# A state-space layer rewritten in chunks of four tokens, its chunk matrices built during the feed-forward network before it

## The chip, the cores and the metric

The kernel runs on one core of one Trainium2 chip. The metric is the device time of one execution in microseconds. The engines are named as the profile names them: PE (TensorE), DVE (VectorE), ACT (ScalarE), POOL (GpSimd) and SP (SyncE, which only issues DMAs here).

## The reference, cut to what matters

Two blocks run one after the other on 256 tokens of width 1024. The second has four layers, each a mixer followed by a SwiGLU feed-forward network (FFN): forgetting attention ("fox"), S5, a pooling layer, fox again. The S5 layer is what the change rewrites:

```
u = h @ w_in                                # 256 x 1024, 64 groups of 16 channels
lam_bar = exp(lam * dt)                     # complex, 64 groups x 64 states
b_bar = ((lam_bar - 1) / lam) * b
bu = b_bar u                                # 16 channels -> 64 states in each group
state_t = lam_bar * state_{t-1} + bu_t      # over the 256 tokens
y = Re(c state) + d * u
g = gelu(y);  val, gate = split(g @ w_glu);  x = x + val * sigmoid(gate)
```

## The kernel before, in words

Activations lie transposed in SBUF, features over the partitions in KC = 8 tiles of 128 rows and T = 256 columns (tokens). Weights stream through two rings of four buffers that SP fills: `ring` with tiles of 1 MB, `dring` with down projections of 0.5 MB. A product of fp32 precision is made of three fp32r matmuls (`mm3`, lines 644 to 646): weights are split into a high half by ACT (`make_high`, line 1248; `make_down_high`, line 1254) and a low half by DVE (`make_low`, line 380; `make_down_low`, line 389). Nothing plans the order at run time: each engine has its own program, and semaphores join them.

An FFN has 22 slices. PE (`swiglu`) issues for slice j first `gate_up(j + 2)`, 48 matmuls, and then `down(j)`, 24 matmuls. ACT's part of slice j is: wait for the scaled sums of j, SiLU (line 1499), `make_high(j + 2)`, `make_down_high(j + 1)`. The last of these waits until PE has done `down(j - 1)`, since there are two buffers:

```
if d >= HIGH or not isinstance(g, int):
    act.wait_ge(sem("down_free"), d - HIGH + 1 + RING * g)
```

DVE scales the sums (line 2099), makes the hidden activations (2102 to 2106), the low half of tile j + 2 and of down tile j + 1, and in slices 1 to 5 of the FFN in front of S5 also a part of `s5_matrices`, which scales B (lines 2269 to 2275, six operations of 256 elements).

The S5 layer: PE projects u with four tiles (`s5in`), DVE scales it (line 2282). Then 32 columns j of 128 states follow. For each, PE multiplies B with u (line 1145, 2 matmuls of 256 tokens), DVE rotates into a frame in which the recurrence is real (lines 2298 to 2302), runs two scans over 256 tokens (line 2306), rotates back (2310 to 2312), leaving the two products of each part apart, and PE sums them in PSUM while it multiplies with C (line 1161, 4 matmuls). Line 1155 adds d * u. The rotations are tables of 256 tokens for four columns, doubled eight times by POOL (`rotations`, lines 591 to 598) in two buffers: the first two are made during the attention of layer 0, the others while the scan runs, each when DVE has left the buffer. After every four columns ACT applies gelu to a tile of 128 outputs (line 1568) and makes its high half (1570), DVE the low half (2315), and PE runs the GLU, 16 groups of 24 matmuls on eight tiles.

## Time and profile before

| | |
|---|---|
| median of 3 runs | 2737.49 us (2734.57 to 2745.36) |
| the profiled execution's own time | 2734.69 us |
| its span in the profile | 2733.0 us |
| busy in the span | PE 2280.9, DVE 1724.9, ACT 1079.3, POOL 735.9 us |
| mean granted clock of PE | 0.90 of full speed |

The profile is one execution. "Busy" is the time in which an engine had an instruction running; a wait is put down to what released it. A clock of 1.00 is 2.4 GHz, 0.50 is 1.2 GHz. The stages around the change follow each other so: attention of layer 0 until about 1438 us, its output projection, FFN0 from 1467 to 1653, the S5 projection until 1682, the scan until 1896, the GLU until 1949.

### The profile page before, as it was taken

The numbers are of one execution on the slowest core, as the hardware profiler recorded it, in microseconds if no ns is written. First come the engines' busy times: TensorE is split into PE (matmuls) and PEld (weight loads), VectorE is DVE, ScalarE is ACT, GpSimd is POOL, SyncE is SP. The second block draws the span as 40 slices with busy tenths as digits, with TensorE's granted clock in tenths as the row PEclk, the third lists the DMA queues.
The fourth block names the chain that finished last, engine by engine and source line by source line (L and its number), as shares of the span: only waits on it lengthen the run. The fifth ranks groups of instructions, "written<-read, shape, count | busy, mean of one in ns | idle before, by whom it ended". The sixth has DMA issues, their size and how long they took to land.

```text
span 2733.0 us, 40794 instructions
## 1 busy us (share of the span) xinstructions
PE 2280.9 (83%) x15156; PEld 1926.7 (70%) x15160; DVE 1724.9 (63%) x2631; ACT 1079.3 (39%) x1527; POOL 735.9 (27%) x522
## 2 busy tenths in 40 slices
PE   5998768688678865875999997667999699999997
PEld 2864545677466555764969996224999599887997
DVE  3488463477458545765557667997666766654665
ACT  3221533376432534664444333001433333445432
POOL 2320032488452135883240000783000000000000
PEclk7995889899788888997999998777999899999999
DMA  5248702499526125995415452000545244442442
GB/s 232 93 185 323 246 0 107 185 341 343 209 77 234 44 88 205 323 321 185 160 42 202 174 208 77 0 0 31 185 184 200 100 162 184 164 152 72 175 184 92
DMA packets 93046, 443.72 MB, mean 162 GB/s; under 512 B 9088, under 2 KB 25600, under 8 KB 56704
## 3 DMA queue, kind: packets, MB, share of 16 engines
q1 hardware_dynamic: 79104, 390.10, 39.1%
q0 software_dynamic: 8496, 31.99, 3.0%
q10 hardware_dynamic: 5328, 20.04, 1.8%
q8 instruction: 76, 1.25, 0.2%
q14 instruction: 42, 0.34, 0.0%
HBM read 401.20 MB, written 40.89 MB: 162 GB/s over the span
## 4 chain that ended last, share of the span: by engine, by line
PE 39%; DVE 6%; POOLq 2%; POOL 2%; ACT 2%; DVEq 2%; issue 1%; DMA 0%; ACTq 0%
PE bank L645 12%; PE bank L644 11%; PE bank L646 11%; DVE ring_halves L380 2%; POOLq L593 1%; ACT high L1248 1%; POOLq L598 1%; PE bank L1098 1%; POOL XT L591 1%; PE bank L1075 1%; PE bank L1088 1%; DVEq L2301 1%; PE bank L1161 1%; POOL XT L594 1%; PE bank L686 1%
## 5 line engine op out<-in xcount | busy, mean ns | idle before, releaser
L644 PE MATMUL bank<-ssdb_halves,high 128*128 128x256 f32 (+1 forms) x2080 | 613.2, 295 | 62.3 <-DVE HT_halves L1683 34.9
L645 PE MATMUL bank<-HT_halves,high 128*128 128x256 f32 (+1 forms) x2096 | 623.7, 298 | 0.0
L646 PE MATMUL bank<-ssdb_halves,ring_halves 128*128 128x256 f32 (+1 forms) x2080 | 612.3, 294 | 0.0
L380 DVE TENSOR_TENSOR ring_halves<-ring,high 128x2048 fp32r<-128x2048 f32 (+1 forms) x200 | 414.8, 2075 | 157.7 <-ACT high L1248 157.5
L1248 ACT CAST high<-ring 128x2048 fp32r<-128x2048 f32 x230 | 437.2, 1903 | 134.1 <-PE bank L646 134.1
L380 POOL TENSOR_TENSOR ring_halves<-ring,high 128x1024 fp32r<-128x1024 f32 (+1 forms) x96 | 363.6, 3789 | 375.3 <-ACT high L1248 375.3
L644 PEld LDWEIGHTS bank<-ssdb_halves,high 128*128 128x128 f32 x2080 | 398.3, 192 | 81.9 <-issue 55.1
L645 PEld LDWEIGHTS bank<-HT_halves,high 128*128 128x128 f32 x2096 | 398.9, 190 | 9.1
L646 PEld LDWEIGHTS bank<-ssdb_halves,ring_halves 128*128 128x128 f32 x2080 | 394.6, 190 | 9.7
L389 DVE TENSOR_TENSOR dring_halves<-dring,dhigh 128x1024 fp32r<-128x1024 f32 (+1 forms) x152 | 226.0, 1487 | 154.7 <-ACT dhigh L1254 148.5
L1254 ACT CAST dhigh<-dring 128x1024 fp32r<-128x1024 f32 x152 | 160.5, 1056 | 238.2 <-PE bank L646 238.1
L644 PE MATMUL bank<-border_halves,dhigh 128*128 128x256 f32 x704 | 198.4, 282 | 9.1 <-DVE border_halves L2106 9.1
L646 PE MATMUL bank<-border_halves,dring_halves 128*128 128x256 f32 x704 | 198.1, 281 | 0.0
L645 PE MATMUL bank<-border_halves,dhigh 128*128 128x256 f32 x704 | 198.0, 281 | 0.0
L646 PE MATMUL bank<-high,HT_halves 128*128 128x256 f32 x640 | 182.7, 285 | 0.0
L644 PE MATMUL bank<-high,HT_halves 128*128 128x256 f32 x512 | 156.8, 306 | 17.9 <-POOL ring_halves L380 11.0
L1161 PE MATMUL bank<-wide,zs_b 128*32 128x256 f32 x256 | 94.5, 536 | 68.0 <-DVE wide L2312 67.9
L645 PE MATMUL bank<-ring_halves,HT_halves 128*128 128x256 f32 x512 | 145.6, 284 | 0.0
L644 PEld LDWEIGHTS bank<-border_halves,dhigh 128*128 128x128 f32 x704 | 133.3, 189 | 9.8 <-issue 9.8
L645 PEld LDWEIGHTS bank<-border_halves,dhigh 128*128 128x128 f32 x704 | 133.4, 189 | 0.0
L646 PEld LDWEIGHTS bank<-border_halves,dring_halves 128*128 128x128 f32 x704 | 133.2, 189 | 0.0
L644 PE MATMUL bank<-HT_halves,high 128*128 128x256 f32 (+1 forms) x384 | 117.9, 307 | 9.5 <-DVE MIX_halves L1903 8.4
(426 smaller groups left out, 4384.1 us busy)
## 6 DMA issues: line engine op xcount, KB each, us to landing
ring<-in_ffn SPq DMA_DIRECT2D x88, 1024.0 KB, 5.4
ring<-in_moe SPq DMA_DIRECT2D x64, 1024.0 KB, 7.5
ring<-in_ada SPq DMA_DIRECT2D x48, 1024.0 KB, 7.0
dring<-in_ffn_down SPq DMA_DIRECT2D x88, 512.0 KB, 3.5
dring<-in_moe_down SPq DMA_DIRECT2D x64, 512.0 KB, 4.6
ring<-in_foxin SPq DMA_DIRECT2D x24, 1024.0 KB, 4.8
ring<-in_win SPq DMA_DIRECT2D x22, 1024.0 KB, 4.8
zs_b<-x_slots POOLq DMA_DIRECT2D x32, 512.0 KB, 8.6
```

The costliest lines, as they stand in the source:

```text
L380: eng.tensor_tensor(low, w, h, ALU.subtract).then_inc(sem(f"low_{engine}"), 1)
L389: eng.tensor_tensor(low, w, h, ALU.subtract).then_inc(sem(f"down_low_{engine}"), 1)
L591: ptt(new, low, cos, ALU.mult)
L593: pool.drain()
L594: ptt(new[:, 0], new[:, 0], tmp[:, 1], ALU.subtract)
L598: pool.drain()
L644: mm(o, a[0], b[0], start=first, stop=last and bool(kw), **kw)
L645: mm(o, a[0], b[1], start=False, stop=last and bool(kw), **kw)
L646: return mm(o, a[1], b[0], start=False, stop=last, **kw)
L1161: i = mm(y, cT[:, part, j, :], z, start=False, stop=n == 3, skip_group_check=True, tile_position=(0, q))
L1248: nc.scalar.copy(r(high[c % HIGH][:]), ring[t % RING][:]).then_inc(sem("high"), 1)
L1254: nc.scalar.copy(r(dhigh[d % HIGH][:]), dring[d % RING][:]).then_inc(sem("down_high"), 1)
```

## The change

The tokens are taken in 64 chunks of four. A state is carried from chunk to chunk only, so a column of 128 states has 64 steps in place of 256, and one DVE instruction now works on four columns at once: there are 8 of them (c), of 256 elements as before. PE forms the input of a chunk from its four tokens with the powers of lam times B (8 matmul calls of 128 weights and 64 columns per c), the outputs of the four tokens from the state before the chunk with C times the powers (8 calls), and what the tokens of a chunk do to each other with a 128 x 128 matrix per column that also holds d (4 calls). DVE adds the two products of the rotation itself (one more addition of 512 elements per c).

The matrices are built in FFN0, whose loops are written out in full on PE, ACT and DVE. In slices 1 to 16 DVE makes one power of B or C per slice (two halves of 16 columns, four steps of B and four of C each), in slices 5 to 8 and 13 to 16 ACT spreads the powers of B into block form and PE transposes them, which ACT copies back, in slices 9 to 12 and 17 to 20 ACT does the same with C and PE multiplies C with B to give the sums inside a chunk. POOL doubles two tables of 64 rotations for 16 columns each (six levels, products of up to 1024 elements), and stores everything with its DMAs in DRAM. In the S5 layer SP loads for each c a tile of 1 MB (B and C) and one of 0.5 MB (the matrix in the chunk and the rotations), and moves u into chunk order and gelu(y) back, in four moves of 16 DMAs of 32 partitions by 1 KB. POOL no longer works during attention and scan; a 32 x 63 product makes the decay (`fade`). The B and C arrays in DRAM are half as large, and the four transposes and ACT copies ahead of the S5 projection and the skip matrix on DVE are gone. Two GLU low halves that DVE made ahead of the scan are made behind it. The first two groups of the GLU are interleaved on PE. ACT does not begin layer 1 before the last matrix is stored.

```diff
+            def s5_moves(t0):
+
+                def tables(c):
+                    if c < RING:
+                        sp.wait_ge(sem("down_free"), DOWN_AT["ffn", 0] + FFN_SLICES)
+                    else:
+                        sp.wait_ge(*at("s5_pe", ("out", c - RING)))
+                    sp.dma_start(dring[c % RING][:], s5_kr[c]).then_inc(*done(f"s5_kr{c % RING}", c, 16))
+                    load(t0 + c, s5_bc[c])
+
+                def move(half, dst, src, key):
+                    for s_ in range(STEP):
+                        for q in range(BATCH):
...
+                            sp.dma_start(dst(s_, q, half), src(s_, q, half)).then_inc(*done(f"moved{half}", key, 16))
...
+                for n in ("s5_bt_kept", "s5_c_kept", "s5_k_kept0", "s5_k_kept1", "s5_loaded"):
+                    sp.wait_ge(*at(n, "last"))
+                for c in range(2):
+                    tables(c)
+                sp.wait_ge(*at("s5_dve", ("u_sb", 3)))
+                move(0, to_rel, from_nat, "u")
+                for c in range(2, RING):
+                    tables(c)
+                sp.wait_ge(*at("s5_dve", ("u_sb", KC - 1)))
+                move(1, to_rel, from_nat, "u")
+                for c in range(RING, KC):
+                    tables(c)
+                sp.wait_ge(*at("s5_act", ("y", 3)))
+                move(0, to_nat, from_rel, "y")
...
+            def s5_keep_out(c):
+                pool.wait_ge(*at("s5_act", ("e_blk", c)))
+                for i in range(2):
+                    pool.dma_start(s5_bc[c][:, (2 + i) * BATCH * P:(3 + i) * BATCH * P].rearrange("p (b c) -> p b c", b=BATCH),
+                                   e_blk[:, i, :, 1:, :].rearrange("p b s c -> p b (s c)"))\
+                        .then_inc(*done("s5_c_kept", c if c < KC - 1 else "last", 16))
...
+                s5_turns(0)
+                for half in range(2):
+                    for c in range(BATCH * half, BATCH * half + BATCH):
+                        s5_keep(c)
+                    if half == 0:
+                        pool.wait_ge(*at("s5_loaded", "rot"))
+                        s5_turns(1)
+                    for c in range(BATCH * half, BATCH * half + BATCH):
+                        s5_keep_out(c)
+                        if c > BATCH * half:
+                            s5_keep_k(c - 1)
+                    s5_keep_k(BATCH * half + BATCH - 1)
@@ PE @@
+                half, c = j // 13, (j - 5) % 4 + 4 * (j // 13)
+                if 5 <= j <= 8 or 13 <= j <= 16:
+                    pe.wait_ge(*at("s5_act", ("x_blk", c)))
+                    for q in range(BATCH):
+                        for i in range(2):
+                            mm_ = nc.tensor.transpose(ps[6 + q // 2][:, (2 * (q % 2) + i) * P:(2 * (q % 2) + i + 1) * P],
+                                                      x_blk[:, i, q].rearrange("p s c -> p (s c)"), ident)
+                    mm_.then_inc(*done("s5_pe", ("turned", c)))
+                c = (j - 9) % 4 + 4 * (j // 17)
+                if 9 <= j <= 12 or 17 <= j <= 20:
+                    pe.wait_ge(*at("s5_act", ("e_blk", c)))
+                    pe.wait_ge(*at("s5_dve", ("e", c // 4)))
+                    for q in range(BATCH):
+                        o = ps[6 + c % 2][0:QUAD, q * P:q * P + P]
+                        for i in range(2):
+                            mm(o, b_one[:, i, (BATCH * c + q) % S5_HALF, :], e_blk[:, i, q, 0:STEP, :], start=q == 0 and i == 0,
+                               stop=False, skip_group_check=True)
+                        mm_ = mm(o[:, 0:QUAD], ident[:, 0:QUAD], skip_diag[:, (BATCH * c + q) % S5_HALF, :], start=False, stop=True,
+                                 skip_group_check=True)
+                    mm_.then_inc(*done("s5_pe", ("k_sums", c)))
...
+                if build is not None:
+                    for j in range(slices):
+                        build(j)
+                        if j + 2 < slices:
+                            gate_up(j + 2, 0)
+                        down(j, 0)
+                    return
...
+                    w = ring[t % RING][:, 0:2 * BATCH * P].rearrange("p (b a s) -> p b a s", b=BATCH, a=2)
                     for i in range(2):
-                        mm_ = mm(ps[j % 2][:, i * T:i * T + T], bT[q:q + 32, i, c, :], Q2[q:q + 32, c, :],
-                                 start=True, stop=True, tile_position=(q, 0))
-                    mm_.then_inc(sem("bu"), 1)
-
-                def outputs(j):
-                    q, c = 32 * (j % 4), j // 4
-                    bank = ps[2 + c % 2]
-                    if j % 4 == 0:
-                        if c >= 2:
-                            pe.wait_ge(*at("s5_y", c - 2))
-                        mm(bank[:, 0:T], s5_dmat[:, c, :], Q2[:, c, :], start=True, stop=False, skip_group_check=True)
-                    pe.wait_ge(sem("states_done"), j + 1)
-                    y = bank[q:q + 32, 0:T]
-
-                    for n, (part, z) in enumerate(((0, s5_q[:, j % 2, 0, 0, :]), (0, s5_q[:, j % 2, 1, 0, :]),
-                                                   (1, s5_q[:, j % 2, 0, 1, :]), (1, s5_q[:, j % 2, 1, 1, :]))):
-                        i = mm(y, cT[:, part, j, :], z, start=False, stop=n == 3, skip_group_check=True, tile_position=(0, q))
-                    i.then_inc(sem("s5_out"), 1)
+                        for q in range(BATCH):
+                            mm_ = mm(ps[c % 2][:, i * T + q * CHUNKS:i * T + q * CHUNKS + CHUNKS], w[:, q, i, :], u_rel[:, q, c, :],
+                                     start=True, stop=True)
+                    mm_.then_inc(*done("s5_pe", ("in", c)))
+
+                def outputs(c):
+                    w = ring[(t0 + c) % RING][:, 2 * BATCH * P:].rearrange("p (a b s) -> p a b s", a=2, b=BATCH)
+                    pe.wait_ge(*at(f"s5_kr{c % RING}", c))
+                    if c < 2:
+                        pe.wait_ge(*at("s5_dve", ("u_sb", KC - 2 + c)))
+                    else:
+                        pe.wait_ge(*at("s5_act", ("y", c - 2)))
+                    y = ps[2 + c % 2]
+                    for q in range(BATCH):
+                        mm(y[:, q * CHUNKS:q * CHUNKS + CHUNKS], dring[c % RING][:, q * P:q * P + P], u_rel[:, q, c, :],
+                           start=q == 0, stop=False, skip_group_check=True)
+                    pe.wait_ge(*at("s5_dve", ("states_done", c)))
+                    for q in range(BATCH):
+                        for part in range(2):
+                            z = s5_q[:, c % 2, 0, part, q * CHUNKS:q * CHUNKS + CHUNKS - 1]
+                            mm_ = mm(y[:, q * CHUNKS + 1:q * CHUNKS + CHUNKS], w[:, part, q, :], z,
+                                     start=False, stop=part == 1, skip_group_check=True)
+                    mm_.then_inc(*done("s5_pe", ("out", c)))
+                    pe.drain().then_inc(sem("tile_free"), 1)
 
                 inputs(0)
-                for j in range(S5_CH):
-                    if j + 1 < S5_CH:
-                        inputs(j + 1)
-                    outputs(j)
+                for c in range(KC):
+                    if c + 1 < KC:
+                        inputs(c + 1)
+                    outputs(c)
@@ ACT @@
+                def turned(c):
+                    act.wait_ge(*at("s5_pe", ("turned", c)))
+                    if c:
+                        act.wait_ge(*at("s5_bt_kept", c - 1))
+                    for i in range(2):
+                        copied = nc.scalar.copy(b_turned[:, 2 * i:2 * i + 2], ps[6 + i][:].rearrange("p (b a s) -> p b a s", b=2, a=2))
...
+                    q = BATCH * (c % BATCH)
+                    for g in range(2):
+                        rows = slice(64 * g, 64 * g + 64)
+                        nc.scalar.copy(x_blk[rows, :, :, :, 16 * g:16 * g + 16].rearrange("p a b s c -> p a (b s) c"),
+                                       x_pow[rows, :, q:q + BATCH].rearrange("p a b s c -> p a (b s) c"))
+                        copied = nc.scalar.copy(b_one[rows, :, q:q + BATCH, 16 * g:16 * g + 16], x_pow[rows, :, q:q + BATCH, STEP - 1, :])
+                    copied.then_inc(*done("s5_act", ("x_blk", c)))
...
+                def out_blocks(c):
+                    act.wait_ge(*at("s5_dve", ("e", c // BATCH)))
+                    if c:
+                        act.wait_ge(*at("s5_pe", ("k_sums", c - 1)))
+                        act.wait_ge(*at("s5_c_kept", c - 1))
+                    q = BATCH * (c % BATCH)
+                    for g in range(2):
+                        rows = slice(64 * g, 64 * g + 64)
+                        nc.scalar.copy(e_blk[rows, :, :, 0, 16 * g:16 * g + 16], e_one[rows, :, q:q + BATCH])
+                        for i in range(2):
+                            copied = nc.scalar.copy(e_blk[rows, i, :, 1:, 16 * g:16 * g + 16], e_pow[rows, i, q:q + BATCH])
+                    copied.then_inc(*done("s5_act", ("e_blk", c)))
+
+                if 6 <= j <= 9 or 14 <= j <= 17:
+                    turned((j - 6) % 4 + 4 * (j // 14))
+                if 10 <= j <= 13 or 18 <= j <= 21:
+                    sums((j - 10) % 4 + 4 * (j // 18))
+                if 5 <= j <= 8 or 13 <= j <= 16:
+                    blocks((j - 5) % 4 + 4 * (j // 13))
+                if 9 <= j <= 12 or 17 <= j <= 20:
+                    out_blocks((j - 9) % 4 + 4 * (j // 17))
...
+                    if build is not None:
+                        build(j)
...
+                    act.wait_ge(*at("s5_pe", ("out", c)))
+                    act_fn(g_rel[:, :, c, :], ps[2 + c % 2][:, 0:T].rearrange("p (b t) -> p b t", b=BATCH), ACT.Gelu_apprx_tanh)\
+                        .then_inc(*done("s5_act", ("y", c)))
+                    if c >= 5:
+                        gelu_high(c - 5)
+                    if c == 6:
+                        make_high(SPLIT_AT["glu", 1])
+                gelu_high(3)
+                make_high(SPLIT_AT["glu", 1] + 1)
+                for c in range(BATCH, KC):
+                    gelu_high(c)
@@ DVE @@
+                def times(x, re, im, out, conj):
+                    f_re, f_im = (pv(i)[:, own].unsqueeze(1).unsqueeze(3).to_broadcast([P, 2, S5_HALF, 16]) for i in (re, im))
+                    a, b = s5_tmp
+                    tt(a, x, f_re, ALU.mult)
+                    tt(b, x, f_im, ALU.mult)
+                    dve.drain()
+                    tt(out[:, 0], a[:, 0], b[:, 1], ALU.add if conj else ALU.subtract)
+                    return tt(out[:, 1], a[:, 1], b[:, 0], ALU.subtract if conj else ALU.add)
...
+                step = j - 1 if j < 9 else j - 9 if j < 17 else 8
...
+                elif step < STEP:
+                    i = times(x_pow[:, :, :, STEP - step, :], 18, 19, x_pow[:, :, :, STEP - 1 - step, :], False)
+                    if step == STEP - 1:
...
+                    q = s5_q[:, c % 2]
+                    if c >= 2:
+                        dve.wait_ge(*at("s5_pe", ("out", c - 2)))
+                    tt(q[:, 0], s5_z, cos2, ALU.mult)
+                    stt(q[:, 1, 0], s5_z[:, 1], -1.0, sin, ALU.mult, ALU.mult)
+                    tt(q[:, 1, 1], s5_z[:, 0], sin, ALU.mult)
+                    dve.drain()
+                    tt(q[:, 0], q[:, 0], q[:, 1], ALU.add).then_inc(*done("s5_dve", ("states_done", c)))
+                make_low(dve, "dve", SPLIT_AT["glu", 1])
+                for c in range(KC):
+                    dve.wait_ge(*at("s5_act", ("gelu_high", c)))
+                    y = y_nat[:, :, c // BATCH, CHUNKS * (c % BATCH):CHUNKS * (c % BATCH) + CHUNKS]
+                    tt(r(by_step(O2r[:, c, :])), y, by_step(H2r[:, c, :]), ALU.subtract).then_inc(*done("s5_dve", ("gelu_split", c)))
+                    if c == BATCH - 1:
+                        make_low(dve, "dve", SPLIT_AT["glu", 1] + 1)
```

## Rows read from the trace of the kernel before

**Rows 1.** Windows: stretch, length, busy us of PE, PEld, DVE, ACT, POOL, clock, DMA share.

```profile
1467.40:1653.10 185.70, 180.46 (x1522) 179.60 (x1521) 125.91 (x158) 69.78 (x65) 0.00 (x0) 1.00 0.47 177
...
1682.40:1895.80 213.40, 140.25 (x403) 61.94 (x401) 194.80 (x298) 9.09 (x17) 131.53 (x192) 0.73 0.01 5
...
1311.60:1437.60 126.00, 117.92 (x794) 98.39 (x793) 62.05 (x127) 54.48 (x120) 45.23 (x68) 0.95 0.27 93
2381.00:2506.00 125.00, 117.88 (x793) 98.58 (x792) 58.43 (x126) 54.41 (x120) 0.00 (x0) 0.95 0.26 93
```

**Rows 2.** Timeline of DVE over the first column: start us, us, engine, line, operation.

```profile
1689.88 0.69 DVE L2298 TENSOR_TENSOR wide<-bank,XT 128x512 f32<-128x512 f32 x1 [2.22 <-PE bank L1145]
1690.49 0.41 DVE L2299 TENSOR_TENSOR wide<-bank,XT 128x256 f32<-128x256 f32 x1
...
1694.83 0.68 DVE L2298 TENSOR_TENSOR wide<-bank,XT 128x512 f32<-128x512 f32 x1
```

**Rows 3.** POOL: tables' last six levels (timeline), and contended products by form.

```profile
1382.52 0.24 POOL L591 TENSOR_TENSOR ssdb<-ssdb,arow 128x32 f32<-128x32 f32 x1
...
1394.69 1.89 POOL L592 TENSOR_TENSOR sig<-ssdb,arow 128x1024 f32<-128x1024 f32 x1
...
1397.95 1.28 POOL L595 TENSOR_TENSOR ssdb<-ssdb,sig 128x512 f32<-128x512 f32 x1
...
L592 POOL TENSOR_TENSOR sig<-XT,arow 128x1024 f32<-128x1024 f32 x3 | 7.0, 2340 | 0.0
```

**Rows 4.** Timeline of PE: the eight output instructions of two columns.

```profile
1882.43 1.91 PE L1161 MATMUL bank<-wide,zs_b 128*32 128x256 f32 x8 [0.31 <-DVE wide L2312]
...
1892.28 3.62 PE L1161 MATMUL bank<-wide,zs_b 128*32 128x256 f32 x8 [1.78 <-DVE wide L2312]
...
1895.84 0.58 PE L644 MATMUL bank<-HT_halves,high 128*128 128x256 f32 x1
```

**Rows 5.** Timeline of DVE: third and fourth u of the S5 projection.

```profile
1670.42 0.75 DVE L2282 TENSOR_TENSOR HT<-bank,rstd 128x256 f32<-128x256 f32 x2
```

**Rows 6.** DMA issues (KB each, us to landing) and timelines of SP and POOL issuing.

```profile
zs_b<-x_slots POOLq DMA_DIRECT2D x32, 512.0 KB, 8.6
...
ring<-in_glu SPq DMA_DIRECT2D x8, 1024.0 KB, 4.8
...
473.05 0.33 SPq L422 DMA_DIRECT2D ring<-in_moe  x1
473.42 0.44 SPq L427 DMA_DIRECT2D dring<-in_moe_down  x1
...
1458.26 0.60 POOL L627 DMA_DIRECT2D MIX<-in_s_b  x1 [59.03 <-DVE XT L1922]
```

**Rows 7.** Timeline of ACT over one slice of FFN0.

```profile
1543.26 1.05 ACT L1254 CAST dhigh<-dring 128x1024 fp32r<-128x1024 f32 x1 [2.95 <-PE bank L646]
1546.46 0.42 ACT L1499 ACTIVATE border<-wide 128x256 f32<-128x256 f32 x1 [2.15 <-DVE wide L2099]
1546.78 1.90 ACT L1248 CAST high<-ring 128x2048 fp32r<-128x2048 f32 x1
1551.76 1.05 ACT L1254 CAST dhigh<-dring 128x1024 fp32r<-128x1024 f32 x1 [3.08 <-PE bank L646]
```

**Rows 8.** FFN0: waits (total us, times, longest); groups by form, 1468 to 1665.

```profile
ACT dhigh L1254 <- PE bank L646: 55.3, 20, 3.2
...
PE bank L644 <- DVE ring_halves L380: 2.9, 2, 1.6
...
L1557 ACT COPY MIX<-bank 128x512 f32<-128x512 f32 x3 | 1.5, 584 | 0.0
```

**Rows 9.** Windows behind two gaps of PE, columns as in Rows 1.

```profile
2389.80:2392.40 2.60, 0.06 (x2) 0.06 (x1) 2.53 (x3) 1.71 (x1) 0.00 (x0) 1.00 0.77 246
2393.00:2396.50 3.50, 3.50 (x19) 3.50 (x18) 1.43 (x1) 0.00 (x0) 0.00 (x0) 0.51 0.13 52
...
1668.00:1671.40 3.40, 0.75 (x6) 0.78 (x7) 3.40 (x5) 1.90 (x1) 0.00 (x0) 1.00 0.67 231
1671.40:1675.00 3.60, 3.60 (x33) 3.60 (x32) 2.40 (x2) 0.00 (x0) 0.00 (x0) 1.00 0.19 77
```

353 lines of the change are left out of this document (206 added, 147 removed).

## The prediction

> **What bounds the kernel now.** I read the stages first, as windows of the span [rows 1]. The first FFN of the second block (FFN0, 1467 to 1653 us) has PE busy 180.5 of 185.7 us: PE is the bound. The stretch from the end of the S5 input projection to the GLU (1682.4 to 1895.8, 213.4 us) has DVE busy 194.8 us, PE 140 at a mean granted clock of 0.73, and POOL 132. There DVE works through 32 columns; undisturbed, one takes 4.95 us from start to start [rows 2], but 32 of them would be 158 us, so some 50 us are waits and contention with POOL, which makes the rotation tables of the next four columns: a contended 1024-element product there takes 2.34 us, a clean one 1.89 [rows 3]. PE's outputs end the stage: 8 matmul instructions in 3.62 us at the low clock, 1.91 at the high one [rows 4], and the GLU starts at 1895.8.
>
> **What goes and what comes.** The scan shrinks from 32 columns to 8 (four tokens per step), and everything a chunk needs (the powers of B and C, the kernel inside a chunk, the 64-step rotations) is built during FFN0 by DVE, ACT, PE and POOL and kept in DRAM. Two costs have to be told apart: the new S5 stage, and FFN0, where the building is put on a stage that PE bounds.
>
> **1. The new S5 stage.** Count from the end of FFN0, 1653.1. Before, the GLU starts at +242.7 [rows 1]. After:
> - PE still projects until about +29 [rows 1]. The first move to chunk order needs the fourth u, which DVE has at 1671.2, +18 [rows 5]; it is 16 small DMAs on SP. Two issues of SP stand 0.37 us apart, one takes 0.33 to 0.44 [rows 6]; at 0.45 each 7.2 us, and a landing of 2.5 to 4 (the nearest, 1 MB, is 4.8 [rows 6]): done at +29, under the projection. First column at +32, against +36.8 before [rows 2].
> - One column on DVE: 4.95 plus a drain and one 512-element addition (0.69, of which 0.61 to the next start [rows 2], and some 0.15 for the drain), so 5.7. PE has 20 matmul calls of 64 columns in it, 40 instructions; 0.11 us each at the high clock is 4.5 us, at the low one 8 to 9 (an estimate: a quarter of the 0.24 and 0.45 per 256 columns of [rows 4], doubled for the load of 128 weights beside so few columns). PE would bind at the low clock only; I take 6.1 per column, 8 of them 49 us. Bounds 5.7 and 8: 46 and 64.
> - Tail, all on the path: last outputs 3, gelu 0.5, the last move 16 x 0.45 = 7.2 and 2.5 to land, ACT's and DVE's splits 2. Less 5 us of GLU matmuls that the two interleaved first groups have done by then. A move bounded by 0.37 and 1.0 per issue is 6 to 16.
> - Sum: 32 + 49 + 3 + 0.5 + 7.2 + 2.5 + 2 - 5 = +91. Saved: 242.7 - 91 = **151.5 us**.
>
> SP is also passed by 12 MB of tables (8 x 1.5 MB). Tables 0 to 3 come under the projection; table c waits for outputs of c - 4 and has four columns, 24 us, to land; 1 MB takes 4.8 [rows 6]. Hidden; if it were not, every column would wait some 2 us. GLU tiles load from the fifth output on, hidden too; the fourth comes behind the last move but has 17 us. The two low halves of GLU tiles that DVE makes ahead of the scan (2.28 each) move behind it, one under the last outputs, one under the last move, where DVE has nothing else. The skip matrix (1.2 us) and the four transposes ahead of the scan go. Fox0's attention loses POOL's tables: that stage was 126.0 against 125.0 for its twin without them [rows 1], gain 1.
>
> **2. FFN0, per slice.** Today a slice is 8.5 us of PE (two ACT casts of dhigh start 1543.26 and 1551.76) [rows 7]. ACT's cast of the next down weights must wait for PE's down(j-1): 55.3 us of such idle [rows 8]. The new helper is called on ACT behind this cast, and on PE directly behind down(j-1), in front of gate_up(j+2). So for j = 5 to 20 PE stands still until ACT has done the cast and its copies. What was slack of ACT becomes a wait of PE. Sixteen times:
> - cast 1.05 [rows 7] plus three hand-overs at 0.1 = 1.35: **21.6 us**.
> - ACT's copies: 512 elements 0.58 [rows 8], 256 0.42, the next starting 0.1 before the end [rows 7]; 128 elements an estimate of 0.25. State blocks 1.5, output blocks 1.8, turned 1.0, sums 0.5: 8 x 1.5 + 8 x 1.8 + 8 x 1.0 + 7 x 0.5 = **38 us**.
> - PE's own: 64 transposes, one instruction of 128 columns each, 0.12 by halving the 0.24 per 256 columns of [rows 4], 8 us; 64 calls of 128 columns (two instructions each) and 32 of 32 columns, 16 us: **24 us**.
> - A single wait for POOL. ACT has one buffer of output blocks and overwrites it in slice 10 only when POOL's DMA of the first one has landed; POOL issues that after the second half's rotations, which it begins after slice 9's turned blocks. They are the six last levels of today's eight, 16.7 us clean (1382.52 to 1399.23), up to 1.24 times as much beside DVE [rows 3], say 19.5; then six DMA issues at 0.57 and a landing. POOL's 512 KB land in 8.6 us in the MoE [rows 6]; I take 4.5 for 256 KB. Blocks free at 2.2 + 0.6 + 19.5 + 3.4 + 4.5 = 30 after down(8); ACT would be there at 17.5 (a slice of 16 and 1.6 for cast and sums): **12.5 us** (6 to 20).
> - The clock. PE would now stand 2.9 to 4.2 us in each of 16 slices. Behind a 2.5 us gap at 2389.8 it ran 3.4 us at 0.51, 1.2 GHz; behind a similar gap at 1668 it stayed at 1.00 [rows 9]. A low stretch costs half of itself, 1.7. Six in ten: **17 us** (0 to 27).
> - DVE: each step (two 512- and two 256-element operations) equals the old ones in slices 1 to 4, which cost 2.9 us of PE [rows 8]. From slice 5 on it lies under the longer slice. Zero net; without that cover 1 us per slice. The loop written out over 22 slices issues the same matmuls, as the other stages that are written out do; zero.
>
> Sum **113 us**. Behind FFN0 ACT waits for the last kernel DMA, 1 us.
>
> The Trainium skill (DMA: Bandwidth & Descriptors, "Anatomy of one DMA — SWDGE (gpsimd) path") gives a DMA of GpSimd about 2.0 us fixed plus its bytes at 436 GB/s, against this change with its 64 moves and 80 stores. By it 256 KB would land in 2.6 us and the POOL wait would be 10.6, which makes the sum 2 us less; no row here shows so small a DMA, and the nearest, 8.6 us for 512 KB, is far above it.
>
> **Total.** -151.5 - 1 + 113 + 1 = -38.5. Against the profiled execution's 2734.7 (span 2733.0) that is 2696; its run lies 2.8 under the median of 2737.5, so **2699 us**.
>
> **Rivals.**
> - *FFN0 hides more.* The clock stays up and POOL's wait is short: 17 + 8 less; the copies overlap better, 5 less. 2669. For: the gap at 1668 did not lower the clock. Against: PE's order is fixed, the cast can't come earlier.
> - *The S5 stage is PE's or SP's.* Columns of 8 us at the low clock (+15) and moves of 1 us per issue (+9, both moves) or late tables (+6): +30, 2729. For: clock 0.73 in this stage today. Against: DVE's 5.7 leaves PE 1 us of slack at the high clock.
> - *Slower: the clock in FFN0.* If PE's standing in each slice keeps it at 1.2 GHz through slices 5 to 20, and not for one stretch of 3.4 us, each slice's 8.5 us of matmuls becomes 17: 16 x 8.5 = 136 in place of 17, 2818. The change turns slower from about 40 us above my sum, which is 23 more low stretches than my ten, two per slice. For: the scan stage ran at 0.73 with PE busy two thirds. Against: here PE works over 10 us on end between two waits, and at 2393 one 3.4 us stretch was enough. The skill's page "TensorE: Matmul & The Clock Gate", section "HAM oscillation — how this bites in real kernels", tells of a loop whose wait in each turn puts PE back to the low clock each time; by that rule all 16 slices pay 1.7, 27 us, and the time is 2709, inside my forecast.
> - *It does not shorten the scan's bound*: the stage is held by table traffic. 12 MB at four times the landing rate of one MB is 58 us, no more than the columns; 2710. Hardly distinct.
>
> **Chances.** Forecast with its neighbourhood (2680 to 2718) 0.55; more hidden (below 2680) 0.18; S5 stage longer (2718 to 2751) 0.18; slower by FFN0's clock 0.09. A measurement of this kernel tells about 0.5% from no change, 14 us: faster below 2723.8 is 0.55 + 0.18 + a third of 0.18 = 0.79; within 0.12; slower 0.09. Range 2660 to 2736: it leaves out a part of the clock rival and a tail on the other side.
>
> **What would show it.** Right: FFN0 some 300 us long, PE idle in slices 5 to 20 in front of the transposes and sums, released by ACT's copies, 3 to 4 us each; one wait of ACT for a DMA near slice 10, 10 us or more; DVE's columns 5.7 to 6.3 us apart, eight of them; 15 us between the last column and the GLU's full pace. Wrong: FFN0 below 270 or above 330 us; columns over 7 us; PE waiting for tiles of the tables.

## The result and the profile after

The kernel after takes 2749.05 us (median of 7 runs, 2745.08 to 2756.84), the kernel before 2737.49: a ratio of 1.0044, 95% interval 1.0025 to 1.0063. The forecast was 2699, faster; the change made the kernel 0.4% slower. The profiled execution took 2745.08 us with a span of 2743.3, against 2733.0 before.

Where it went, by the reciprocals that open a stage (rstd, VectorE's timeline), the first slice of FFN0 and its last matmul (1653.1 before, 1787.1 after):

| stretch | before | after | difference | forecast |
|---|---|---|---|---|
| start to rstd of fox0 | 1311.65 | 1305.64 | -6.0 | 0 |
| to rstd of FFN0 | 155.7 | 155.2 | -0.6 | -1 |
| FFN0, first slice to last matmul | 182.7 | 323.3 | +140.6 | +113 |
| from there to the S5 rstd | 12.6 | 12.4 | -0.2 | +1 |
| S5 rstd to rstd of FFN1 | 287.2 | 157.8 | -129.4 | -151.5 |
| the rest | 780.0 | 786.0 | +5.9 | 0 |

The first and the last line (work that the change leaves alone) cancel; why each moved by 6 us is not shown. The change saves 129.4 us in the S5 stage and pays 140.6 for it in FFN0.

Windows of the kernel after, columns as in [rows 1]: FFN0, the scan from its first column to just before the last outputs, and the last move.

```profile
1463.80:1787.10 323.30, 242.96 (x1754) 233.62 (x1752) 159.74 (x201) 106.33 (x168) 87.36 (x123) 0.83 0.41 140
1819.80:1885.00 65.20, 60.18 (x287) 58.93 (x285) 42.92 (x80) 4.38 (x10) 0.00 (x0) 0.53 0.53 185
1889.00:1903.00 14.00, 5.75 (x26) 5.45 (x26) 5.57 (x7) 5.36 (x9) 0.00 (x0) 0.62 0.30 84
```

In FFN0 PE is busy three quarters of the time at 0.83, where it was busy 97% of the time at 1.00 [rows 1]. In the scan it is busy 92% of the time at the low clock. The waits of FFN0 name what PE stands for:

```profile
ACT dhigh L1389 <- PE bank L759: 140.6, 19, 11.5
...
PE bank L1105 <- ACT XT L1671: 45.8, 8, 21.1
...
PE bank L1095 <- ACT wide L1658: 28.1, 8, 3.7
...
ACT XT L1669 <- DMA s_bc<-XT: 17.6, 1, 17.6
```

PE waits 16 times for ScalarE's copies, ahead of the transposes (L1095) and the sums (L1105), and one of the 16, 21.1 us, holds ScalarE's wait for GpSimd's store. Summed over PE's timeline, and with each stretch's granted clock from the trace, FFN0 parts into three terms (before: 5.2 us of gaps, nothing at the low clock, 177.5 of work):

| FFN0 | after | against before | forecast |
|---|---|---|---|
| PE stands (18 gaps) | 80.3 | +75.1 | 21.6 + 38 + 12.5 = 72.1 |
| half of PE's 80.8 us of work at 1.2 GHz | 40.4 | +40.4 | 17 (0 to 27) |
| the rest, as at 2.4 GHz | 202.5 | +25.1 | 24 |

Behind one of these stops (3.70 us, at 1560.3) PE runs on without a pause, and the clock is low over most of the first window:

```profile
1564.10:1567.90 3.80, 3.80 (x21) 3.80 (x22) 3.03 (x7) 1.72 (x2) 0.00 (x0) 0.60 0.94 314
1568.00:1574.80 6.80, 6.80 (x59) 6.80 (x58) 2.29 (x1) 0.39 (x1) 0.00 (x0) 1.00 0.02 10
```

Beside 18 gaps there were 17 such low stretches, 112.6 us in all (what of it lies in gaps included), ten of them 6.8 us long, six 3.4, and one of 23.9 us that covers most of the longest stop. The scan's columns: VectorE's first operation of two columns, and then PE's groups by form from 1838 to 1885 (busy us, mean ns).

```profile
1851.33 0.69 DVE L2524 TENSOR_TENSOR wide<-bank,dring 128x512 f32<-128x512 f32 x1 [3.34 <-PE bank L1274]
1860.36 0.69 DVE L2524 TENSOR_TENSOR wide<-bank,dring 128x512 f32<-128x512 f32 x1 [3.34 <-PE bank L1274]
```

```profile
L1293 PE MATMUL bank<-wide,ring 128*128 128x63 f32 x82 | 18.7, 421 | 0.0
L1274 PE MATMUL bank<-MIX,ring 128*128 128x64 f32 x80 | 18.2, 423 | 1.3 <-issue 1.3
...
L1287 PE MATMUL bank<-MIX,dring 128*128 128x64 f32 x47 | 11.3, 422 | 0.3 <-issue 0.3
```

A column is 9.03 us, and VectorE waits 3.34 of them for PE. 18.7 / 82 is 0.228 us per instruction (they overlap, so the mean of one is longer), times 40 is 9.1: PE's instructions at the low clock are the whole column. The last move, SP's issues and PE's wait behind them:

```profile
1889.48 10.01 SPq L513 DMA_DIRECT2D XT<-zs_b  x16
```

```profile
PE bank L757 <- DVE MIX_halves L2546: 8.0, 1, 8.0
```

### The profile page after: what moved, and what is told of

Same layout as the page of the kernel before. It is cut to its first block, busy times and chain, and to the rows that moved or that the text cites. A ratio compares the mean times of both kernels' runs of the same rounds, so it can differ in the third digit from the quotient of the medians.

```text
span 2743.3 us, 40602 instructions
## 1 busy us (share of the span) xinstructions
PE 2273.3 (83%) x15320; PEld 1992.1 (73%) x15320; DVE 1615.0 (59%) x2468; ACT 1116.0 (41%) x1627; POOL 653.0 (24%) x391
## 3 DMA queue, kind: packets, MB, share of 16 engines
q1 hardware_dynamic: 84480, 404.79, 41.8%
## 4 chain that ended last, share of the span: by engine, by line
PE 43%; DVE 4%; ACT 3%; issue 2%; DVEq 1%; POOL 1%; DMA 0%; SPq 0%; POOLq 0%; ACTq 0%
PE bank L757 12%; PE bank L759 12%; PE bank L758 11%; DVE ring_halves L401 2%; PE bank L1293 1%; PE bank L1105 1%; PE bank L1274 1%; ACT high L1383 1%; PE bank L1241 1%; PE bank L1218 1%; PE bank L1231 1%; PE bank L1095 1%; PE bank L1223 1%; PE bank L799 0%; PE bank L1222 0%
## 5 line engine op out<-in xcount | busy, mean ns | idle before, releaser
L757 PE MATMUL bank<-ssdb_halves,high 128*128 128x256 f32 (+1 forms) x2080 | 626.3, 301 | 66.8 <-DVE HT_halves L1887 34.8
L759 PE MATMUL bank<-ssdb_halves,ring_halves 128*128 128x256 f32 (+1 forms) x2080 | 621.8, 299 | 0.0
L758 PEld LDWEIGHTS bank<-HT_halves,high 128*128 128x128 f32 x2096 | 408.8, 195 | 9.4
L759 PEld LDWEIGHTS bank<-ssdb_halves,ring_halves 128*128 128x128 f32 x2080 | 403.1, 194 | 9.8
L759 PEld LDWEIGHTS bank<-high,HT_halves 128*128 128x128 f32 x640 | 124.0, 194 | 0.0
```

The lines of the kernel that those rows point to most:

```text
L757: mm(o, a[0], b[0], start=first, stop=last and bool(kw), **kw)
L758: mm(o, a[0], b[1], start=False, stop=last and bool(kw), **kw)
L759: return mm(o, a[1], b[0], start=False, stop=last, **kw)
```

## The experiments

**e1_build_late: PE works gate_up(j+2) ahead of the build.**

```diff
-                        build(j)
                         if j + 2 < slices:
                             gate_up(j + 2, 0)
+                        build(j)
                         down(j, 0)
```

> The kernel after, with one edit: in slices 5 to 20 of the first FFN of block 1 (FFN0), TensorE works gate_up(j+2) first and then the build of chunk kernels, in place of the other way round. Theory (TensorE stands still because its build is in front of gate_up and has to wait for ScalarE's cast and copies, and each stop is followed by a stretch at 1.2 GHz): with some 7 us of matmuls between down(j-1) and the build, the copies are done when the build comes; the 16 gaps of 2.7 to 3.9 us go to under 1 us (-40 us or more), most of the low stretches go too (-15 or more); FFN0 from its first to its last slice falls from 311.6 to 240 to 260 us, the kernel to about 2690. Rival A (the build's own work on TensorE and on ScalarE is the bound, and the gaps only show it): FFN0 stays above 295 us. Rival B (only the gaps go, the clock stays low): 265 to 275 us, mean granted clock of slices 5 to 20 below 0.85.

Measured: 2673.13 us, ratio 0.9762 (0.9730 to 0.9795). FFN0 from first to last slice 236.5 us (311.6 in the kernel after; this measure, which the expectations use, ends at the last slice's scaled sums, 11.7 us ahead of the last matmul that closes the 323.3 us above). That is a little below the theory. Its window to the last matmul, and PE's waits:

```profile
1465.70:1713.60 247.90, 212.54 (x1753) 207.98 (x1752) 156.30 (x201) 106.58 (x168) 86.03 (x123) 0.93 0.54 182
```

```profile
PE bank L1105 <- ACT XT L1671: 20.7, 1, 20.7
PE bank L757 <- DVE ring_halves L401: 11.3, 8, 3.8
```

PE works the same instructions and, up to the last slice, waits once for ScalarE in place of 15 times. Gaps 35.4 us (80.3 after), the low clock's price 8.5 (40.4), the work at the high clock 204.0 (202.5). So 45 us of the 75 gained were stops and 32 were the clock behind them; both rivals fall. The one wait left has grown to 22.8 us on ScalarE: faster slices reach it earlier, GpSimd doesn't.

**e2_tables_first: GpSimd makes both halves of the rotations ahead of its stores.**

```diff
                 s5_turns(0)
+                pool.wait_ge(*at("s5_loaded", "rot"))
+                s5_turns(1)
                 ...
-                    if half == 0:
-                        pool.wait_ge(*at("s5_loaded", "rot"))
-                        s5_turns(1)
```

> The kernel after, with GpSimd computing both halves of the rotations before it stores the first blocks of FFN0, in place of storing between the halves. Theory (one single wait of 17.6 us of ScalarE, for GpSimd's store of the first output block, which stands behind the second half of the rotations): that wait goes; FFN0 311.6 to 294 to 300 us. Rival (the blocks come free no earlier, since the second half of rotations is on GpSimd before slice 10 either way and other copies then wait): 308 us or more, with a wait of ScalarE of 10 us or more for a store elsewhere.

Measured: FFN0 297.9 us from first to last slice (-13.7; one time, 2735.59). ScalarE has no wait for a store left, as the theory has it; 4 us of the 17.6 came back as a longer stop in slice 5 (PE's longest wait for the transposes 6.9 us, before 3.7) with the low clock behind it: GpSimd's second half now runs until 1533.5, just ahead of that stop, and VectorE's operations stretch beside it.

**e3_filler and e4_pe_sums: the clock and VectorE's addition in the scan.** e3 adds, between inputs(c + 1) and outputs(c):

```diff
+                    for n in range(4):
+                        mm(ps[6][:], zeros[:, 0:P], zeros, start=True, stop=True)
```

> The kernel after, with four matmuls of zeros over 512 columns added to each column of the scan on TensorE, between the next column's inputs and this column's outputs; nothing reads them. The 8 columns stand 9.03 us apart with TensorE busy 92% of the time at a granted clock of 0.53. Theory (the columns are long since TensorE runs its 64-column matmuls at 1.2 GHz though it has hardly any gap; wider matmuls would raise the clock): columns 6 to 7 us apart at a clock near 1.0, the scan 15 to 20 us shorter, in spite of the added work. Rival (the clock stays at 0.5 whatever is issued; the work alone counts): 4 x 0.43 = 1.7 us more per column, 10.7 us apart, the scan 12 to 14 us longer.

Measured: from the fourth column on 5.72 us apart, the S5 stage 139.9 us (157.8 after), one time of 2732.29. A window in it, and two columns:

```profile
1850.00:1875.00 25.00, 23.73 (x191) 21.24 (x189) 23.16 (x43) 4.46 (x7) 0.00 (x0) 1.00 0.72 260
```

```profile
1851.01 0.69 DVE L2526 TENSOR_TENSOR wide<-bank,dring 128x512 f32<-128x512 f32 x1
1856.73 0.69 DVE L2526 TENSOR_TENSOR wide<-bank,dring 128x512 f32<-128x512 f32 x1
```

PE does more and the stage is 18 us shorter. VectorE waits for nothing and sets the 5.72, the forecast's 5.7.

e4 takes away VectorE's addition and lets PE sum all four products:

```diff
-                            z = s5_q[:, c % 2, 0, part, ...]
-                            mm_ = mm(..., stop=part == 1, ...)
+                            for k_ in range(2):
+                                z = s5_q[:, c % 2, k_, part, ...]
+                                mm_ = mm(..., stop=part == 1 and k_ == 1, ...)
 ...
-                    dve.drain()
-                    tt(q[:, 0], q[:, 0], q[:, 1], ALU.add)
```

> The kernel after, with the last step of the change's title undone: TensorE sums all four products of a rotation (16 calls of 63 or 64 columns per column for the outputs, in place of 8), and VectorE's drain and addition of 512 elements go. Theory (TensorE at 1.2 GHz bounds the columns: 9.2 us of its instructions in 9.03 us): 8 more calls at 0.45 us make 12.6 us per column, the scan 28 us longer in all. Rival (VectorE is the bound and the change's addition costs): columns 0.8 us shorter, 8.2, the scan 6 us shorter. Third: with twice the work TensorE's clock rises and the columns stay at 8 to 10 us.

Measured: 12.44 us per column, the S5 stage 184.7, one time of 2772.09 us. PE bounds, and busy 98% of the time it still has the low clock:

```profile
1850.00:1885.00 35.00, 34.22 (x159) 33.75 (x159) 14.04 (x27) 1.15 (x3) 0.00 (x0) 0.50 0.37 127
```

**e8_sums_filler: both edits.**

> e3_filler together with e4_pe_sums: the kernel after, with TensorE summing all four products and the four matmuls of zeros per column. It tells what VectorE's addition is worth once the clock is up (columns 5.72 us apart with it). Theory (at the high clock TensorE's instructions take half as long: 12.44 / 2 = 6.2 us of its own per column plus 0.85 of zeros, against 4.95 for VectorE without its addition): columns 6.8 to 7.3 us apart, so the addition on VectorE is worth 1.1 to 1.6 us per column even then. Rival (TensorE hides the eight calls more at the high clock, VectorE bounds): 5.0 to 5.4 us, the addition a loss of 0.5 us per column.

```profile
1862.16 0.69 DVE L2527 TENSOR_TENSOR wide<-bank,dring 128x512 f32<-128x512 f32 x1 [2.58 <-PE bank L1274]
1869.66 0.69 DVE L2527 TENSOR_TENSOR wide<-bank,dring 128x512 f32<-128x512 f32 x1 [2.58 <-PE bank L1274]
```

Measured: 7.50 us apart, VectorE waiting 2.58 for PE; 0.2 above the theory's span (one time, 2749.04). VectorE's addition is worth 12.44 - 9.03 = 3.4 us per column at the low clock and 7.50 - 5.72 = 1.8 at the high one. So the addition on VectorE is a gain at either clock.

**e5_three: e1, e2 and e3 together.**

> The edits of e1_build_late, e2_tables_first and e3_filler together on the kernel after. Theory (three causes that add: gaps and clock in FFN0, one wait for GpSimd's store, the clock in the scan): FFN0 from first to last slice 212 to 220 us (236.5 less the slice of 32.9 that shrinks to 11 to 13), the S5 stage from its rstd to that of the next FFN 140 us, the kernel 2630 to 2640. Rival (with shorter slices GpSimd's stores can't keep pace, and ScalarE's wait for them comes back in each slice): FFN0 above 228 us, the kernel 2645 or more. Against the kernel before, FFN0 then still carries 35 to 43 us for the build, and the S5 stage is some 147 us shorter.

Measured: 2645.33 us, ratio 0.9633 (0.9596 to 0.9669). FFN0 222.1 us, a little over the theory's span; to its last matmul it has 20.4 us of gaps and 9.5 for the clock. GpSimd keeps pace, so the rival falls, though the kernel's time is the 2645 that it named. The S5 stage took 159.7 us, where the theory had 140: in the profiled execution the zeros did not bring the clock back until the seventh and last distance between columns:

```profile
1752.98 0.69 DVE L2525 TENSOR_TENSOR wide<-bank,dring 128x512 f32<-128x512 f32 x1 [4.94 <-PE bank L1273]
1763.61 0.69 DVE L2525 TENSOR_TENSOR wide<-bank,dring 128x512 f32<-128x512 f32 x1 [4.94 <-PE bank L1273]
```

10.63 us per column, e3's rival almost to the number. One edit showed both outcomes; runs of this kernel spread from 2635.81 to 2658.45.

**e6_k_buffer: e5 without ScalarE's wait for the last stores.**

```diff
-        k_blk = [view(wide, 1536 + 512 * i, BATCH, P) for i in range(2)]
+        k_blk = [view(sigf, 512 * i, BATCH, P) for i in range(2)]
 ...
-                if i_layer == 1:
-                    for i in range(2):
-                        act.wait_ge(*at(f"s5_k_kept{i}", "last"))
```

> e5_three with ScalarE's two blocks for the kernels inside a chunk placed in the buffer that the rotations used before (free by then), so that ScalarE no longer waits, behind FFN0, for their last stores before it splits the input of the S5 projection. Theory (that wait stands on the path: 24.1 us from the last slice to the S5 rstd where the kernel before had 18.0): 18 us again, the kernel 6 us below e5_three. Rival (the table transfers on SyncE's queue, which wait for the same stores, come late instead): the first column of the scan starts 3 us or more later after the rstd than 20.4, and the kernel gains less than 3 us.

Measured: 2641.43 us, ratio 0.9646 (0.9611 to 0.9681), the same as e5. The stretch from the last slice to the S5 rstd stayed at 24.1. Neither the theory nor the rival holds: the first column came 20.3 us behind the rstd, no later. What failed is the premise that ScalarE's wait alone stood on the path. PE's stop in slice 20 lies there too, and e9, e12 and e13 below show what lies beside it. PE's last matmul came 11.7 us behind the last slice in the kernel after, 5.4 before. Here, too, ScalarE waits for VectorE and that for PE:

```profile
ACT ssdb_halves L1433 <- DVE XT L2337: 6.2, 3, 5.8
...
PE bank L1104 <- ACT XT L1672: 3.4, 1, 3.4
```

**e7_split_move: e5 with half of the last move on GpSimd's queue.**

```diff
-                for s_ in range(STEP):
+                for s_ in range(STEP // 2):
```

(on SP; the same loop from STEP // 2 on stands in GpSimd's program behind the build, with a semaphore of its own)

> e5_three with eight of the sixteen transfers of the last move (from chunk order to channel order ahead of the GLU) on GpSimd's queue, which is idle there, in place of SyncE's. Theory (the move is on the path, 10.0 us for 16 issues at 0.62 us): the time from the last column's outputs to the first new GLU matmul falls by 4 to 5 us. Rival (GpSimd's transfers land 2 us or more later than SyncE's, or the move's data and not its issues is the limit): less than 2 us gained.

```profile
1799.81 4.95 SPq L513 DMA_DIRECT2D XT<-zs_b  x8
```

```profile
1800.08 3.96 POOL L749 DMA_DIRECT2D XT<-zs_b  x8 [100.09 <-ACT zs_b L1772]
```

Measured: 2643.64 us, ratio 0.9631 (0.9599 to 0.9662); the timed runs can't tell it from e5. In the stage it shows: from the eighth column's start to the rstd of FFN1 71.7 us, in e3, e5 and e6 76.2, 77.0 and 76.2. The issues were the limit, 4.5 to 5.3 us.

**e9_all: more zeros at the start of the scan, and the build of slice 20 behind down(20).** Both on e7.

```diff
+                for n in range(14):
+                    mm(ps[6][:], zeros[:, 0:P], zeros, start=True, stop=True)
                 inputs(0)
 ...
-                    for n in range(4):
+                    for n in range(8 if c < 2 else 4):
 ...
-                        build(j)
+                        if j != slices - 2:
+                            build(j)
                         down(j, 0)
+                        if j == slices - 2:
+                            build(j)
```

> e7_split_move with two edits. First, more matmuls of zeros where TensorE waits at the start of the scan: 14 ahead of the first column's inputs, 8 in the first two columns, 4 in the others as before. In four executions with 4 in each column the clock rose in the columns 3, 3, 4 and 6. Theory (it is the waiting in the first columns that lets the clock fall, and 4 wide matmuls are only just enough to bring it back): the clock stays at 1.0 from the first or second column on, all 8 columns span 38 to 41 us (59.4 in the profile of e7_split_move, 42.1 in the best of the four). Rival (the rise is chance): 50 us or more. Second, the build of slice 20 goes behind down(20) instead of ahead of it, since no gate_up is left to hide ScalarE's copies there. Theory: the 6 us that the stretch from the last slice to the S5 rstd is longer than before (24.1 against 18.0, which e6_k_buffer showed not to be the wait for the last stores) are this gap of 3.6 us and the low clock behind it; it falls to 19 to 20. Rival: it stays at 23 or more. The kernel: 2615 to 2630 us.

Measured: 2637.68 us, ratio 0.9608 (0.9594 to 0.9622), above the expected span. (The expectation misreads the traces in part: the clock rose in the third column in e3 and e6, the sixth in e7 and the seventh in e5, and the seven distances were 58.3 us in e7 and 41.8 in e6, not 59.4 and 42.1.) The seven distances between columns came to 44.3 us: the clock was still up at the first column but fell at 1742 for 10.2 us, behind a gap of 1.5. Neither reading of the columns holds. The stretch to the S5 rstd: 23.8, PE's gap gone, nothing gained, as the second rival has it.

**e10_short_turns: GpSimd's rotations without their last two levels** (the rotations from the 16th chunk on are left out).

```diff
-                for n in range(6):
+                nc.gpsimd.memset(rot[:, :, :, 16:], 0.0)
+                for n in range(4):
```

> The kernel after without the last two of the six levels of GpSimd's rotations in both halves (a memset fills their place), so the rotations from the 16th chunk on are not computed. It prices GpSimd's products in FFN0. Theory (VectorE's operations of slices 1 to 3 stretch, one of 256 elements from 0.42 to 1.98 us, while GpSimd works its levels of 256 to 1024 elements, and TensorE waits for the split weights 2.6 and 3.8 us; the forecast had zero for this): the slices 1 to 4, now 10.9, 14.7, 8.9 and 11.7 us, come to 42 us or less together in place of 46.2, and the wait of ScalarE for the first output block falls from 17.6 us to 7 or less, since the second half is 12 us or more shorter; FFN0 311.6 to 292 to 299 us. Rival (VectorE's stretch comes from elsewhere, as from the DMA traffic or from more of its own work): slices 1 to 4 stay within 1 us of 46.2.

In the kernel after, VectorE's 256-element subtraction and addition of slice 2, beside GpSimd's products of 1024:

```profile
1488.90 1.98 DVE L2476 TENSOR_TENSOR zs_b<-wide 128x256 f32<-128x256 f32 x1
1490.81 2.13 DVE L2477 TENSOR_TENSOR zs_b<-wide 128x256 f32<-128x256 f32 x1
```

```profile
1488.42 2.18 POOL L664 TENSOR_TENSOR ssdb<-ssdb,arow 128x1024 f32<-128x1024 f32 x1
1490.57 2.10 POOL L665 TENSOR_TENSOR sig<-ssdb,arow 128x1024 f32<-128x1024 f32 x1
```

and the same without those levels:

```profile
1486.41 0.42 DVE L2477 TENSOR_TENSOR zs_b<-wide 128x256 f32<-128x256 f32 x1
1486.75 0.42 DVE L2478 TENSOR_TENSOR zs_b<-wide 128x256 f32<-128x256 f32 x1
```

Measured: slices 1 to 4 39.7 us (46.2 after, 38.0 before), ScalarE's wait for the first output block 10.0, FFN0 297.3, one time of 2728.56. The theory holds but for the wait, 3 us above its bound. Of the 8.2 us that slices 1 to 4 had grown by, 6.5 are gone.

**e11_before_filler: two matmuls of zeros in each of the 32 columns of the kernel before.**

> The kernel before, with two matmuls of zeros over 512 columns in each of its 32 columns of the scan. It asks whether the low clock of TensorE (0.73 in that stage) cost the kernel before as it costs the kernel after. Theory (VectorE bounds those columns at 4.95 us, TensorE waits for it): the stage from rstd to rstd, 287.2 us, changes by less than 6 us, and the ratio to the kernel before lies within 0.998 and 1.002; so what the low clock costs is a cost of the change alone. Rival (outputs at the low clock end columns there too): 10 us or more shorter.

Measured: ratio 0.9988 (0.9976 to 1.0001), the stage from rstd to rstd 285.5 us against 287.2. The clock there went only from 0.73 to 0.76. The theory's numbers hold and the rival's 10 us did not come, but what a clock of 1.00 would give the kernel before is not shown; with VectorE busy 194.8 of the 213.4 us of the scan [rows 1] it could be little while VectorE's work stays as it is.

**e12_both: e9 with e6's buffer.**

```diff
-                    for n in range(8 if c < 2 else 4):
+                    for n in range((8, 14, 8)[c] if c < 3 else 4):
```

(and e6's diff)

> e9_all with the block buffer of e6_k_buffer, so that ScalarE's wait for the last stores behind FFN0 is gone too; and 14 matmuls of zeros in the second column, 8 in the third. e6_k_buffer took away that wait and e9_all took away TensorE's gap in front of the last build, and neither shortened the stretch from the last slice to the S5 rstd (24.1 and 23.8 us, before 18.0). Theory (each hid the other: ScalarE's wait ends at the same time as TensorE with the gap): with both gone the stretch is 18 to 20.5 us. Rival (a third thing holds it, as SyncE's tables or VectorE's contention with DMAs there): 23 us or more. The scan's 8 columns: 7 distances in 40 to 42 us where the clock stays up (46.6 in e9_all, where it fell in the second and third column), 46 or more where the zeros don't hold it. The kernel 4 to 10 us below e9_all.

Measured: 2644.32 us, ratio 0.9654 (0.9629 to 0.9679). The kernel was to be 4 to 10 us below e9 and is not: against the kernel before, its ratio lies above e9's and the intervals don't meet; what costs the 0.5% stays open. The stretch is 22.2 us, 1.6 below e9: neither reading. The distances between columns came to 46.4 us (e9's were 44.3, not the 46.6 that the expectation has), the clock low for 10.2 us again, so the zeros don't hold it. VectorE's timeline, and GpSimd's beside it, show something else in that stretch:

```profile
1698.40 3.68 DVE L1915 SCALAR_TENSOR_TENSOR HT_halves<-XT,vec,ssdb_halves 128x256 fp32r<-128x256 f32 x1 [0.24 <-ACT ssdb_halves L1445]
```

```profile
1698.23 3.56 POOL L724 TENSOR_TENSOR ssdb<-s5p 128x2016 f32<-128x2016 f32 x1
```

**e13_fade_late: e12 with that product of GpSimd moved.**

```diff
+                pool.wait_ge(*at("s5_dve", ("u_sb", 3)))
                 nc.gpsimd.memset(fade[:, :, 0:1], 0.0)
```

> e12_both with one edit: GpSimd makes the decay factors of the scan (one product of 2016 elements, 3.56 us) behind VectorE's fourth u of the S5 projection, in place of as soon as the stores of FFN0 are issued. In e12_both this product runs from 1698.23 to 1701.79, and VectorE's first norm product of the next stage (256 elements, two sources in SBUF) starts at 1698.40 and takes 3.68 us, where its seven fellows take 0.47; in e9_all it takes 2.13 and ends 0.3 behind GpSimd's product too. Theory (VectorE stands until GpSimd's product is through, and this was the third cause behind the two of e6_k_buffer and e9_all): all eight take under 0.6 us, and the stretch from the last slice to the S5 rstd falls from 22.2 to 18 to 19.5 us. Rival (the long product has another cause, as the read of a block that comes late): the stretch stays at 21.5 or more. The first column of the scan may start no later than before, 21 to 24 us behind the rstd.

```profile
1699.52 0.49 DVE L1916 SCALAR_TENSOR_TENSOR HT_halves<-XT,vec,ssdb_halves 128x256 fp32r<-128x256 f32 x1 [0.25 <-ACT ssdb_halves L1446]
```

```profile
1717.16 5.40 POOL L725 TENSOR_TENSOR ssdb<-s5p 128x2016 f32<-128x2016 f32 x1
```

```profile
1716.88 2.28 DVE L401 TENSOR_TENSOR ring_halves<-ring,high 128x2048 fp32r<-128x2048 f32 x1
```

Measured: 2636.4 us, ratio 0.9625 (0.9603 to 0.9647). The stretch is 18.4 us, before 18.0; the product of VectorE takes 0.49. Now GpSimd's product is the longer one, 5.40, where VectorE's 2.28 us low half of a tile (the last line) had begun first. So the 6 us behind FFN0 had three causes, each ready to take the place of the others: PE's gap in the last build, ScalarE's wait for stores, and GpSimd's product (in the kernel after it ends at 1787.05, ahead of VectorE's first norm product at 1788.24, and costs nothing yet). One or two taken away gave 0 to 2 us, all three 5.7.

## Why the prediction was wrong, step by step

**FFN0, the stops: right.** 21.6 + 38 + 12.5 = 72.1 forecast, 75.1 measured: the build's 16 stops without ScalarE's wait 56.3 (59.6 forecast), that wait 17.6 (12.5), the other gaps 6.4 against 5.2 before. The wait's 5 us more are not GpSimd's rotations, which took 19.4 us (19.5 forecast): it stood 5.7 us ahead of their first product, and the profile names no releaser for that. PE's own work: 24 forecast, 25.1 measured.

**FFN0, the clock: the first step that failed.** The step was "Six in ten: 17 us", from two gaps [rows 9]: behind one the clock fell for 3.4 us, behind the other it did not. Here 17 low stretches came with the 18 gaps, and most were 6.8 us long: 40.4 us, beyond the upper bound of 27. e1 took the stops away and the price fell to 8.5, so it hangs on the stops. The rule of the Trainium skill cited in the forecast (TensorE: Matmul & The Clock Gate, "HAM oscillation — how this bites in real kernels"), that each turn of such a loop pays, agrees with this trace (a low stretch with 15 of the build's 16 stops), as the 0.6 did not; the 27 us that I worked out by it were still 13 short.

**FFN0, VectorE: "Zero net" failed.** Slices 1 to 4 took 8.2 us more (46.2 against 38.0), in gaps and in the low clock behind them, so it is in the terms above. I had counted VectorE's elements, and knew contention only as the 1.24 of [rows 3]. That factor is a mean over products as long as GpSimd's own; a short operation caught behind a long product of GpSimd takes the long one's time: 1.98 for 0.42, 3.68 for 0.48. e10 and e13 show it by taking the long one away. A page that the forecast had not drawn on states it: in the Trainium skill, SBUF — State Buffer, section "SBUF: two separate sides", the port pair that GpSimd and VectorE share is an exclusive lock, held for a whole instruction. These rows agree.

**Behind FFN0:** "1 us" for ScalarE's wait; none was paid, since GpSimd's last store came no later than PE. Once PE was faster it came (in e9 ScalarE waits 4.5 us for that store, and VectorE 1.8 us for ScalarE).

**The S5 stage: the columns failed.** The first came 32.7 us behind FFN0's end (32 forecast), and the move with the splits took 12.6 (11.7). From the first column to the start of the last move it was 69.6 us, where 49 + 3 + 0.5 stood. The price of a column at the low clock, "8 to 9", was right: 9.03. What failed was the step "I take 6.1 per column", near the high clock's value, for which the forecast gives no reason though it had read a clock of 0.73 in today's scan. PE was 92% busy and was not granted the high clock, nor when 98% busy in e4. e3's 5.72 at a clock of 1.00, with more work on PE, shows that the clock made the difference. Of the 5 us of GLU matmuls done ahead 2 came back (GLU to the rstd of FFN1: 57.1 before, 55.2 after): PE spent 4.8 us on 21 of these matmuls at the low clock, where 21 take 2.5 us at the high one.

**The rivals.** Two of them came true together, "the clock in FFN0" by a fifth of its size (+23 of 119) and "the S5 stage is PE's" in its columns (+17 for its +15). I had given them 0.09 and 0.18 as alternatives. The total is off by 48.8 us of span (+10.3 against -38.5): 23 clock in FFN0, 17 columns, 4 in FFN0's other terms, and 4 in small ones behind. Neither rival alone would have turned the result; both are prices of PE's low clock, neither excludes the other, and so they should have been added. Of the signs of being wrong one came, columns over 7 us; FFN0 stayed below the 330 us of the other. The table-traffic rival speaks of "four times the landing rate of one MB", but its 58 us are 12 MB at that rate itself (12 x 4.8); no column waited for a table.

Of the change's idea nothing fell. With PE's build behind gate_up the same work is 2.4% faster than the kernel before, and with the other edits 3.8% (e9: 0.9608; e13: 0.9625). In the kernel before, e11's two matmuls per column gained nothing that could be measured (0.9988), at a clock that rose only to 0.76.

## What to carry to other kernels

When extra work for another engine is threaded into a stage that PE bounds, put PE's share behind the longest piece of PE work that doesn't depend on it: here one moved line was worth 75 us, more than 40% of it in clock. Price the clock as a cause of its own, once for all stages that it touches, and add the cases that share it. And where a delay stays after its cause is taken away, look for the next one behind it before calling the theory dead: three hid each other here.

## What the runs showed of the hardware that was not expected

- PE with instructions of 63 or 64 columns in fp32 stayed at 1.2 GHz while busy 92% (clock 0.53) and 98% (0.50) of a window. With four matmuls of 512 columns in each column of the scan the clock rose to 1.00, but not surely: the seven distances between columns were 43.4, 62.3, 41.8 and 58.3 us in the four profiled executions with the same four (e3, e5, e6, e7), and 44.3, 46.4 and 46.4 in the three with more (e9, e12, e13). What decides between them stays open.
- An operation of VectorE with two sources in SBUF stood until GpSimd's was through (3.68 us for 0.48), and GpSimd's until VectorE's was (5.40 for 3.56).
- Small moves cost by their issues: 0.62 us each on SyncE, 0.5 on GpSimd.
